# Differential-attention units in a two-layer decoder: pT copy ahead of the exponential, the causal mask as a matmul, and two blocks of products interleaved with the units

## The reference, cut to what matters

```python
# 12 query/key heads of 64 (rotary applied), in 6 pairs; v has 6 heads of 128; blocks of 128 queries
s = einsum('bqhd,bkhd->bhqk', q_block, k) * d ** -0.5
s = where(kpos <= qpos, s, -inf)
p = softmax(s).reshape(B, H, 2, Q_BLOCK, S)
a = p[:, :, 0] - lam * p[:, :, 1]           # lam = exp(lq1.lk1) - exp(lq2.lk2) + lambda_init
o = einsum('bhqk,bkhe->bqhe', a, v)         # then rmsnorm per head * g_subln * (1 - lambda_init)
m = memory_attention(q_mem, mem, w_mem_kv)  # 4 heads over 256 memory rows
mixed = concat([o, m]) @ w_out              # 1024 x 1024, then the residual
```

## Time and profile before

| what | value |
|---|---|
| median of 3 runs | 1555.04 us (1552.46 to 1555.53) |
| the profiled execution: its own time, and its span | 1555.01 us, 1553.1 us |
| PE busy, PEld busy | 1478.3 us (95%), 1250.2 us (80%) |
| DVE busy, ACT busy | 1152.5 us (74%), 962.6 us (62%) |
| mean granted TensorE clock | 0.966 of full speed |
| chain that ended last, by engine | PE 91%, DVE 4%, ACT 3%, issue 2% |

### The profile page before, as it was taken

The page is one execution under the profiler, slowest core; times in us unless marked ns, Lnnn a source line. Parts: engine busy times, 40 slices in busy tenths (PEclk is TensorE's granted clock), DMA queues, the critical chain, the costliest instruction groups (busy, mean ns, idle before and its releaser), DMA issues.

```text
span 1553.1 us, 19922 instructions
## 1 busy us (share of the span) xinstructions
PE 1478.3 (95%) x7534; PEld 1250.2 (80%) x7534; DVE 1152.5 (74%) x942; ACT 962.6 (62%) x884; POOL 11.5 (1%) x24
## 2 busy tenths in 40 slices
PE   7988899998996799999999999999999999999996
PEld 7975799997875578888888888888888888888885
DVE  4554544446667389879879879979988987987985
ACT  4652443344555286677767768677768677766773
POOL 1000000000000000000000000000000000000000
PEclk9995899999997899999999999999999999999998
DMA  9750245545431179989989999998997997997990
GB/s 306 249 170 28 95 163 200 181 165 204 147 109 55 41 262 387 392 289 387 392 295 376 397 335 329 393 359 313 396 384 285 394 392 293 388 393 283 388 386 31
DMA packets 201043, 428.34 MB, mean 276 GB/s; under 512 B 8864, under 2 KB 42816, under 8 KB 200992
## 3 DMA queue, kind: packets, MB, share of 16 engines
q1 hardware_dynamic: 199856, 424.18, 74.7%
q0 software_dynamic: 1136, 3.47, 0.8%
HBM read 426.57 MB, written 1.05 MB: 275 GB/s over the span
## 4 chain that ended last, share of the span: by engine, by line
PE 91%; DVE 4%; ACT 3%; issue 2%; DMA 0%; DVEq 0%; SPq 0%; ACTq 0%
PE ps L1349 27%; PE ps L1351 27%; PE ps L1350 27%; PE ps L1759 2%; PE ps L1803 2%; DVE w_lo L837 1%; PE ps L1490 1%; PE ps L1375 1%; ACT w_hi L462 1%; PE ps L1466 1%; PE ps L1543 0%; PE ps L1782 0%; PE ps L1783 0%; PE ps L1550 0%; PE ps L1474 0%
## 5 line engine op out<-in xcount | busy, mean ns | idle before, releaser
L1272 DVE TENSOR_TENSOR e_wlo<-raw,e_whi 128x2048 fp32r<-128x2048 f32 x336 | 750.4, 2284 | 94.0 <-ACT e_whi L773 94.0
L773 ACT ACTIVATE e_whi<-raw 128x2048 fp32r<-128x2048 f32 x336 | 619.9, 1915 | 39.4 <-PE ps L1351 39.3
L1349 PE MATMUL ps<-e_whi,act_hi 128*128 128x512 f32 x1344 | 528.4, 393 | 3.4 <-DVE act_lo L1285 1.9
L1351 PE MATMUL ps<-e_wlo,act_hi 128*128 128x512 f32 x1344 | 523.8, 390 | 0.0
L1350 PE MATMUL ps<-e_whi,act_lo 128*128 128x512 f32 x1344 | 523.2, 389 | 0.0
L1349 PEld LDWEIGHTS ps<-e_whi,act_hi 128*128 128x128 f32 x1344 | 252.4, 188 | 56.5 <-issue 3.1
L1351 PEld LDWEIGHTS ps<-e_wlo,act_hi 128*128 128x128 f32 x1344 | 252.3, 188 | 53.3
L1350 PEld LDWEIGHTS ps<-e_whi,act_lo 128*128 128x128 f32 x1344 | 252.5, 188 | 51.0
L837 DVE TENSOR_TENSOR w_lo<-raw,w_hi 128x2048 fp32r<-128x2048 f32 (+2 forms) x68 | 148.6, 2198 | 145.7 <-ACT w_hi L462 145.4
L462 ACT ACTIVATE w_hi<-raw 128x2048 fp32r<-128x2048 f32 (+2 forms) x68 | 124.0, 1839 | 66.0 <-PE ps L1351 57.9
L778 ACT ACTIVATE act_hi<-ps 128x512 fp32r<-128x512 f32 x56 | 33.6, 599 | 191.9 <-PE ps L1803 191.8
(11 more groups left out here) (225 smaller groups left out, 1111.7 us busy)
## 6 DMA issues: line engine op xcount, KB each, us to landing
raw<-in_w_exp_gate_dram SPq DMA_DIRECT2D x112, 1024.0 KB, 7.5
raw<-in_w_exp_up_dram SPq DMA_DIRECT2D x112, 1024.0 KB, 8.0
raw<-in_w_exp_down_dram SPq DMA_DIRECT2D x112, 1024.0 KB, 8.2
raw<-in_w_dense_gate_dram SPq DMA_DIRECT2D x11, 1024.0 KB, 5.2
raw<-in_w_dense_up_dram SPq DMA_DIRECT2D x11, 1024.0 KB, 5.2
raw<-in_w_dense_down_dram SPq DMA_DIRECT2D x11, 1024.0 KB, 5.4
raw<-in_w_out_dram SPq DMA_DIRECT2D x8, 1024.0 KB, 4.9
raw<-in_w_in_a_dram SPq DMA_DIRECT2D x7, 1024.0 KB, 9.8
```

Of the source, the lines that this page charges most:

```text
L773: nc.scalar.activation(e_whi[:, (s - NPRE) % E_SPLIT, :], raw[:, s % RAW, :], ACT.Copy)\
L1272: nc.vector.tensor_tensor(e_wlo[:, r, :], raw[:, s % RAW, :], e_whi[:, r, :].bitcast(F32), ALU.subtract).then_inc(lo_ready, 1)
L1349: nc.tensor.matmul(dst, l_hi, r_hi, start=start, stop=False)
L1351: return nc.tensor.matmul(dst, l_hi, r_lo, start=False, stop=stop)
```

## The change

Six things move, all in layer 1's attention.

1. On ScalarE `unit_copy(i-2)` stands ahead of `unit_exp(i)`.
2. VectorE no longer adds the causal mask to the scores (`tensor_tensor` on PSUM, L893). TensorE adds it: after each score matmul of a differential unit a matmul of the identity with the mask block (128x128, float32) accumulates into the last 128 columns.
3. The differential units start earlier: the steps D0 to D0+3 stand between the half blocks of `v1`.
4. `memory_out(0)` and `memory_out(1)` stand behind steps D0+6 and D0+8, and their weights' neighbours are split at steps D0+4 and D0+9 (before: before the units, at D0, and at D0+4).
5. The keys' rotary is cut in three pieces: heads 0 to 3 of each tile (128x256 operations, from the first key block alone), then heads 4 and 5 of both tiles together. Each gets a PSUM bank of its own.
6. The three small operations on `lam` move up on VectorE, ahead of the split of slot k+3. At the end `unit_out(U-2)` stands before `head_norm(0)`, and `heads_turn(0)` behind all units' transposes and values.

Accumulators and banks:

```diff
-        ACC_BANK = {(0, 0): 4, (0, 1): 1, (1, 0): 2, (1, 1): 5}
+        ACC_BANK = {(0, 0): 6, (0, 1): 7, (1, 0): 4, (1, 1): 5}
...
-            b = ((0, 1) if u < D0 else (6, 0))[u % 2]
-            return ps[:, b, 0:2 * unit_keys(u)].rearrange("p (i n) -> p i n", i=2)
+            return ps[:, u % 2, 0:2 * unit_keys(u)].rearrange("p (i n) -> p i n", i=2)
 
         def unit_turn_bank(u):
-            return ps[:, 2 + u % 2 if u < NU0 else 2 if u < D0 else 3, :]
+            return ps[:, 2 + u % 2 if u < NU0 else 2, :]
 
         def unit_value_bank(u):
-            return ps[:, 4 + u % 2 if u < NU0 else 3 if u < D0 else 7, 0:P]
+            return ps[:, 4 + u % 2 if u < NU0 else 3, 0:P]
```

ScalarE, the unit loop:

```diff
-            for i in range(D0, U):
+            for i in range(D0 + 4, U):
+                unit_copy(i - 2)
                 unit_exp(i)
-                if i - 2 >= D0:
-                    unit_copy(i - 2)
-                if i - 4 >= D0:
-                    unit_square(i - 4)
+                unit_square(i - 4)
                 if i == D0 + 4:
+                    split_to(o + 3)
+                if i == D0 + 9:
                     split_to(o + 4)
```

VectorE, `unit_max`, the order around `lam`, and the loop:

```diff
-                if units[u][0] == "diff":
-                    last = scores[:, :, unit_keys(u) - P:unit_keys(u)]
-                    m = cst[:, C_CAUSAL:C_CAUSAL + P].rearrange("p (o n) -> p o n", o=1).to_broadcast([P, 2, P])
-                    link(nc.vector.tensor_tensor(last, last, m, ALU.add))
...
-            rope(q_raw, 1, 1, 20)
+            rope(q_raw, 1, 20)
+            dve.wait_ge(lam_a, 1)
+            link(nc.vector.tensor_tensor(lamc[:, 4:5], lamc[:, 3:4], lamc[:, 2:3], ALU.subtract))
+            link(nc.vector.tensor_scalar(lamc[:, 5:6], lamc[:, 4:5], -LAMBDA_INIT, None, ALU.add))
+            link(nc.vector.tensor_scalar(gsub[:, :], gsub[:, :], 1.0 - LAMBDA_INIT, None, ALU.mult))
+            split_to(k + 4)
+            rope(k_raw, 2, 21)
+            unit_max(NU0)
             split_to(k + 5)
-            unit_max(NU0)
             unit_max(NU0 + 1)
             unit_prob(NU0)
...
-            for i in range(D0, U + 1):
+            for i in range(D0 + 3, U + 1):
                 if i < U:
                     unit_max(i)
-                if i == D0:
+                unit_prob(i - 1)
+                unit_out(i - 3)
+                if i == D0 + 4:
+                    dve.wait_ge(mem_hi, 1)
+                    nc.vector.tensor_tensor(act_lo[:, 6:8, :], ps[:, 7, :].rearrange("p (k n) -> p k n", k=2),
+                                            act_hi[:, 6:8, :].bitcast(F32), ALU.subtract).then_inc(mem_lo, 1)
                     split_to(o + 3)
-                if i - 1 >= D0:
-                    unit_prob(i - 1)
-                if i - 3 >= D0:
-                    unit_out(i - 3)
-                if i == D0 + 4:
+                if i == D0 + 9:
                     split_to(o + 4)
```

TensorE, the masked scores, the order behind the first half block of `k1`, and the loop:

```diff
+                masked = kind == "diff"
                 for i in range(2):
-                    ins = nc.tensor.matmul(scores[:, i, :], unit_query(u, i), unit_key(u, i), start=True, stop=True)
+                    ins = nc.tensor.matmul(scores[:, i, :], unit_query(u, i), unit_key(u, i), start=True, stop=not masked)
+                    if masked:
+                        ins = nc.tensor.matmul(scores[:, i, unit_keys(u) - P:unit_keys(u)], ident,
+                                               cst[:, C_CAUSAL:C_CAUSAL + P], start=False, stop=True)
...
+            half_block(k1, 6, 0, 0, kv)
+            pe.wait_ge(rope_out, 2)
+            pe.wait_ge(q_zero, 6)
+            unit_step(NU0)
+            half_block(k1, 6, 0, 1, kv)
+            pe.wait_ge(proj_out, N_IN_A + 5)
+            rope_turn(2)
+            unit_step(NU0 + 1)
+            pe.wait_ge(proj_out, N_IN_A + 4)
+            half_block(k1, 7, 1, 0, kv)
+            unit_step(NU0 + 2)
+            half_block(k1, 7, 1, 1, kv)
+            pe.wait_ge(proj_out, N_IN_A + 6)
+            rope_turn(3)
+            unit_step(NU0 + 3)
+            pe.wait_ge(rope_out, 3)
+            half_block(v1, 4, 0, 0, kv)
+            unit_step(D0)
+            half_block(v1, 4, 0, 1, kv)
+            pe.wait_ge(proj_out, N_IN_A + 8)
+            rope_turn(4)
+            pe.wait_ge(rope_out, 4)
+            unit_step(D0 + 1)
+            half_block(v1, 5, 1, 0, kv)
+            unit_step(D0 + 2)
+            half_block(v1, 5, 1, 1, kv)
+            unit_step(D0 + 3)
...
-            for i in range(D0, U + 3):
+            for i in range(D0 + 4, U + 3):
+                if i == D0 + 6:
+                    pe.wait_ge(proj_out, N_IN_A + 10)
+                if i == D0 + 8:
+                    pe.wait_ge(rope_out, 5)
                 if i < U:
                     unit_scores(i)
-                if D0 <= i - 2 < U:
+                if i - 2 < U:
                     unit_turn(i - 2)
-                if i - 3 >= D0:
-                    unit_values(i - 3)
-                if i == D0 + 1:
+                unit_values(i - 3)
+                if i == D0 + 6:
+                    pe.wait_ge(mem_lo, 1)
+                    w_mem = take()
+                    memory_out(0, w_mem)
+                if i == D0 + 8:
                     memory_out(1, w_mem)
-                if i == U:
-                    pe.wait_ge(u_exp, U)
-                    heads_turn(0)
+            heads_turn(0)
```

More of the change, by code:

```diff
@@ L350, in rope_banks @@
                 return ps[:, 2 * r, :], ps[:, 2 * r + 1, 0:256]
-            return (ps[:, 6, :], ps[:, 7, 0:256]) if r == 2 else (ps[:, 0, :], ps[:, 7, 256:512])
+            return ps[:, 2 + r, :], None
         def heads_bank(part):
-            two, one = ((0, 6), (7, 3))[part]
+            two, one = ((0, 1), (2, 3))[part]
             return ps[:, two, :], ps[:, one, 0:S]
@@ L1612, in rope_turn @@
                 pe.wait_ge(roped, r + 1)
-                for m in range(DH):
-                    dst = four[:, P * m:P * m + P] if m < 4 else two[:, P * (m - 4):P * (m - 4) + P]
-                    ins = nc.tensor.transpose(dst, rot[:, t, P * m:P * m + P], ident)
                 if r < 2:
+                    for m in range(DH):
+                        dst = four[:, P * m:P * m + P] if m < 4 else two[:, P * (m - 4):P * (m - 4) + P]
+                        nc.tensor.transpose(dst, rot[:, t, P * m:P * m + P], ident)
                     for m in range(2):
```

122 lines of the change are left out of this document (61 added, 61 removed).

## The result

The changed kernel takes 1557.56 us (median of 11 runs, 1555.24 to 1559.23), the kernel before on the same chip 1554.09 (11 runs). The ratio is 1.0022, 95% interval 1.0012 to 1.0031: 3.5 us slower. The forecast was 1553.7: 1.3 us faster, too little to be told from no change. Its profiled execution took 1555.76 us with a span of 1554.0.

The account below looks back on a forecast made before the run. TensorE was taken to bind the first stretch, and turn-taking of three engines the second. The terms put the first head product at 505.7 against 506.52 us; with half a microsecond given back, 1.3 earlier: 1553.7 us, range 1549.5 to 1558.5.

Parts of the forecast that it names:

- the pause for `lam`: At TensorE's second half block of `k1`: a new wait for VectorE's low part, 3.8 us, bounds 3.2 to 4.4.
- the lower clock behind it: Behind the pause for `lam`: TensorE products at half speed for a while, costing 1.7 us (0 to 3.4).
- the masks: Mask additions moved to TensorE: 0.46 us each, from below 0.23 to above 0.9.
- a stop at the first split: Unit loop, split at D0+4: ScalarE 1.9, then VectorE 2.3 with reduction and probabilities queued behind; TensorE pauses 4.1 us.
- the first rival: Pauses don't bring the clock down, or the splits hide better: 1549.5 us, chance 0.25.
- the second rival: Lower level persists in the unit loop behind the first split's stop, masks making TensorE the bound: 1562.0 us, chance 0.15.
- the 3.4 counted: Lower-level time already allowed behind the first split's stop: 3.4 us at half speed, costing 1.7 us.
- 3.4 us a pair.: Unit loop: TensorE's time for a pair of steps at 2.4 GHz, in place of 5.69 us.
- 9.8 + 5.6 + 4.1 + 1.7 = 21.2: Loop from D0+4 through the scores of D0+9: steps and scores, both memory products, split's stop, lower clock.
- Behind it the clock: 1.7 again.: Behind the first split's stop in the unit loop: the lower clock costs 1.7 us once more.
- Sum 8.0: From the last exponentials to the first head product: square and copies 0.6, table load to heads' transposes 3.8, the rest 3.6 us.
- the half microsecond given back: Taken off the whole sum for small gaps rounded up and steps overlapping the clock's recovery: 0.5 us.

Follow-up runs that it names:

- e1_lam: Changed kernel with VectorE's wait for the exponentials of `lam` and the three small operations put back behind the second memory unit's output; 1551.09 us.
- e9_splitstep: Changed kernel with both low parts of the unit loop a whole step later on VectorE, early `lam` wait left in; 1548.81 us.
- e3_copy: Kernel before with one edit: ScalarE's copy of unit i-2 ahead of the exponentials of unit i; 1551.45 us.
- e11_expfirst: Changed kernel with exponentials of unit i ahead of the copy of unit i-2 again, over ScalarE's last eight units; 1560.16 us.
- e5_lamsplit: Changed kernel with the `lam` wait put back and both low parts of the unit loop a whole step later on VectorE; 1544.09 us.

## Why the prediction was wrong

The forecast's sum put the first head product 1.3 us earlier than before, and it came 2.4 us later behind the first scores, by the means of four profiles. The waits and the clock behind them were all there: the pause for `lam` (3.52 us and 3.87 of delay; forecast 3.8), the lower clock behind it, the loop's start (40.7 us behind the first scores; forecast 467.0, which is 40.9), the masks (0.22 us a matmul in the timeline, 0.45 a unit), and a stop at the first split (4.22; forecast 4.1). The lower level came behind the pause and behind the first stop, against the first rival, and in the loop it lasted 3.5 or 7.0 us. That is never the 10 and more that the second rival has at its full length, but 7.0 is 3.6 beyond the 3.4 counted, past the mark of about 3 us from which, the prediction said, that rival decides. So in two of the four profiles a part of it came true, at 1.5 us each. What failed is the size of four terms, and all four erred to one side. The forecast put the head product at 505.2 us, a stage of 79.1, 1.3 us shorter than the profile of before. Four profiles of each kernel say 2.4 us longer, which leaves 3.7 to explain:

- **"3.4 us a pair."** Measured from the scores of D0+4 to those of D0+6 470.39 - 466.70 = 3.69 before the stop and 491.06 - 487.17 = 3.89 behind it. Over the loop 0.8 us: 21.97 us where 9.8 + 5.6 + 4.1 + 1.7 = 21.2 stood.
- **"Behind it the clock: 1.7 again."** Right in the first and third profile. In the second and fourth the scores of D0+7 start 1.5 us later (56.0 and 56.1 us behind the first scores instead of 54.5 and 54.9): the lower level lasted twice as long. Mean over four, 0.8 us.
- **"Sum 8.0", and the half microsecond given back.** The last stretch took 8.36 and 8.51 us, and what I took off for rounding up wasn't there: 0.9 us.
- **The base.** The profiled execution stood at the median by its total, so I took its stage for typical. It was the slowest of four by 1.5 us: its unit loop ran at the lower level for most of the way (clock 0.61), the other three less (0.64, 0.83 and 0.63 in the pair behind the stop and 1.00 in the next, where it had 0.50 and 0.79). A stage of 79.1 compared with a usual 78.9 is no gain at all. It is chance, too, that the two first profiles alone (80.43 and 80.52) show no difference: a slow one of before stands beside the fastest of after.

The four make 4.0, and 0.2 goes off for a loop that starts at 40.7 and not 40.9. The step "behind it both kernels do the same matmuls, so the change is worth what it moves this start" held within the spread.

The forecast also asked too little of its own two big terms. The pause for `lam` was priced rightly and accepted as a cost of the change; e1_lam shows it costs 6.5 us of median, which is more than the whole loss. The split's stop was read as "It stays a stop, since the high part sits behind the exponentials and the low part ahead of the next reduction". That is true of the low part, and e9_splitstep shows that it was 8.75 us for two lines. The like stop of the kernel before is 5.72 or 5.73 us long in its three other profiles, not the 4.09 of the earlier trace rows. The gain of the new order of copy and exponential, which the change is named for, is about 2.6 us in either kernel (e3_copy, e11_expfirst).

## What to carry to other kernels

Before pricing an ordering against a chain of waits, look which clock the chain ran at: divide it into the turn-taking and the clock, since a new order takes away the first, and what it does to the clock has to be measured. When an in-order engine gets long, not urgent work (2.3 us of a weight's low part) inside a tight loop, put it behind the short operations that others wait for, not ahead; and when a wait is moved up an in-order engine's program, price everything behind it. Where a stage holds pauses that bring the clock down, take several profiles of the unedited kernel before comparing anything at 0.2%, and compare profiles that show the lower level in the same places.

## What was not expected of the hardware

The same program shows the lower clock level in different places and lengths from one execution to the next: the first unit's scores start between 425.48 and 429.23 us in four profiles of the kernel before, its stage takes 77.35 to 80.43 us, and that of the changed kernel 80.52 to 82.07, with granted clocks of 0.92 and 0.85 in the same stretch with the same 99 instructions. The same pause of 1.94 us had the lower level behind it in three profiles of before and not in the fourth. The stretch behind it is open to the same: the router to the gather took 3.50 + 5.24 us at 0.84 and 0.93 in the first profile of before, and 4.90 + 6.20 at 0.59 and 0.70 in that of after, where the gather and what follows it then ran faster (6.81 us against 8.21):

```profile
536.40:539.90 3.50, 3.40 (x24) 2.24 (x24) 0.78 (x3) 1.49 (x2) 0.00 (x0) 0.84 0.15 59
539.90:545.14 5.24, 1.57 (x12) 1.39 (x12) 3.88 (x26) 3.50 (x3) 0.00 (x0) 0.93 0.00 0
545.14:553.35 8.21, 6.71 (x32) 6.52 (x33) 5.86 (x6) 2.35 (x4) 0.00 (x0) 0.63 0.58 201
```
```profile
536.10:541.00 4.90, 4.74 (x24) 2.77 (x24) 0.82 (x4) 1.49 (x2) 0.00 (x0) 0.59 0.10 33
541.00:547.20 6.20, 2.57 (x13) 2.39 (x13) 3.85 (x26) 3.80 (x3) 0.00 (x0) 0.70 0.00 0
547.20:554.01 6.81, 5.31 (x32) 5.12 (x33) 5.85 (x6) 2.04 (x3) 0.00 (x0) 0.77 0.48 156
```

The last stretch of the stage runs at 0.50 in both profiles of after shown and in e5_lamsplit, whose loop was at 1.00 and the stretch between, with the second stop in it, at 0.91: the dense loop doesn't carry the higher level into it.
